# Block 2's gates: two more slots as three float32r products, and half of the states' turn back on GpSimd

## The reference, cut to what matters

```
h = rms_norm(x, mix_norm)
q_a, k_a, v_a, q_i, k_i, w_i, u_s, q_m, gates = split(h @ w_in)
...
bur, bui = einsum(u, bbr), einsum(u, bbi)          # inputs of the states
_, _, xr, xi = associative_scan(complex_affine, (ar, ai, bur, bui))
y = einsum(xr, c_re) - einsum(xi, c_im) + d * u
...
g = sigmoid(gates)                                 # 256 x 3 x 1024
merged = g[0] * o_a + g[1] * o_b + g[2] * o_m
```

## Time and profile before

| | |
|---|---|
| median of the runs | 2154.79 us (2153.62 to 2156.51) |
| the profiled execution | 2158.26 us, its span 2156.3 us |
| TensorE busy | 2119.3 us, 98% |
| VectorE, ScalarE, GpSimd busy | 74%, 56%, 8% |
| VectorE, low parts of the gates (L3084) | 2.29 us each |
| VectorE, turn of four states | six instructions of 1.22 us |
| VectorE, eight scans | 4.77 us |

### The profile page before, as it was taken

How to read it: one execution, slowest core, us unless ns; L and a number is a source line. 1 busy time by engine, 2 the same in 40 slices (tenths; PEclk the granted TensorE clock), 3 DMA queues, 4 the chain that set the end, 5 groups by cost and what they waited for, 6 DMA issues and landing times.

```text
span 2156.3 us, 31393 instructions
## 1 busy us (share of the span) xinstructions
PE 2119.3 (98%) x11893; PEld 1774.7 (82%) x11893; DVE 1588.5 (74%) x1653; ACT 1217.9 (56%) x1210; POOL 170.6 (8%) x240
## 2 busy tenths in 40 slices
PE   9999999999899999999999999999999999989998
PEld 8987888898788888888888888888788887877887
DVE  3676553567698989989898989989865539866454
ACT  4154443315477777777777777777664423664443
POOL 1200000320200000000000000000166010000000
PEclk9999999999999999999999999999999999999999
DMA  9134555523499999999999999999845564435562
GB/s 364 61 99 157 185 194 175 153 64 102 136 376 371 359 379 371 366 378 363 371 364 372 364 375 368 366 378 361 327 156 187 188 186 156 157 108 164 187 194 79
DMA packets 244409, 542.31 MB, mean 251 GB/s; under 512 B 20214, under 2 KB 122656, under 8 KB 243936
## 3 DMA queue, kind: packets, MB, share of 16 engines
q1 hardware_dynamic: 238896, 521.37, 67.4%
q0 software_dynamic: 4448, 13.79, 2.3%
q10 hardware_dynamic: 976, 5.91, 0.7%
HBM read 538.64 MB, written 2.36 MB: 251 GB/s over the span
## 4 chain that ended last, share of the span: by engine, by line
PE 92%; DVE 6%; ACT 1%; issue 1%; DMA 0%; DVEq 0%; SPq 0%; ACTq 0%
PE bank L1492 9%; PE bank L1493 9%; PE bank L1496 9%; PE bank L1339 9%; PE bank L1341 9%; PE bank L1340 9%; PE bank L1065 6%; PE bank L1520 5%; PE bank L1519 5%; PE bank L1524 5%; PE bank L1063 2%; PE bank L1658 2%; PE bank L1478 1%; PE bank L1132 1%; PE bank L1360 1%; PE bank L1151 1%
## 5 line engine op out<-in xcount | busy, mean ns | idle before, releaser
L2464 DVE TENSOR_TENSOR weights_lo<-ring_data,weights_hi 128x2048 fp32r<-128x2048 f32 x336 | 759.9, 2289 | 81.4 <-ACT weights_hi L2135 80.3
L2135 ACT ACTIVATE weights_hi<-ring_data 128x2048 fp32r<-128x2048 f32 x336 | 639.9, 1920 | 183.5 <-DMA ring_data<-in_moe_w 182.6
L1492 PE MATMUL bank<-weights_hi,xg_hi 128*128 128x512 f32 x896 | 351.6, 392 | 0.0
L1493 PE MATMUL bank<-weights_hi,xg_lo 128*128 128x512 f32 x896 | 348.9, 389 | 0.0
L2459 DVE TENSOR_TENSOR weights_lo<-ring_data,weights_hi 128x2048 fp32r<-128x2048 f32 x98 | 226.5, 2341 | 49.4 <-ACT weights_hi L1910 49.4
L1496 PE MATMUL bank<-weights_lo,xg_hi 128*128 128x512 f32 x896 | 239.8, 389 | 0.0
L1340 PE MATMUL bank<-weights_lo,xT_hi 128*128 128x512 f32 x584 | 230.2, 394 | 0.0
L1339 PE MATMUL bank<-weights_hi,xT_hi 128*128 128x512 f32 x520 | 206.9, 398 | 1.5 <-DVE xT_lo L2452 0.6
L1341 PE MATMUL bank<-weights_hi,xT_lo 128*128 128x512 f32 x520 | 203.8, 392 | 0.0
L1496 PEld LDWEIGHTS bank<-weights_lo,xg_hi 128*128 128x128 f32 x896 | 168.2, 188 | 35.1
L1493 PEld LDWEIGHTS bank<-weights_hi,xg_lo 128*128 128x128 f32 x896 | 168.3, 188 | 34.0
(11 more groups left out here) (524 smaller groups left out, 3181.8 us busy)
## 6 DMA issues: line engine op xcount, KB each, us to landing
ring_data<-in_moe_w SPq DMA_DIRECT2D x672, 512.0 KB, 4.6
ring_data<-in_ffn_w_in SPq DMA_DIRECT2D x88, 512.0 KB, 4.5
ring_data<-in_w_in SPq DMA_DIRECT2D x71, 512.0 KB, 4.3
ring_data<-in_ffn_w SPq DMA_DIRECT2D x66, 512.0 KB, 4.2
ring_data<-in_ffn_w_out SPq DMA_DIRECT2D x44, 512.0 KB, 4.0
ring_data<-in_w_out SPq DMA_DIRECT2D x24, 512.0 KB, 4.6
ring_data<-in_w_in SPq DMA_DIRECT2D x8, 396.0 KB, 4.2
ring_data<-in_w_in SPq DMA_DIRECT2D x8, 390.0 KB, 5.3
```

The costliest lines, as they stand in the source:

```text
L1492: mm(o, xg_hi[:, k, :], e_hi(at)[:, r], start=k == 0, stop=False)
L1493: mm(o, xg_lo[:, k, :], e_hi(at)[:, r], start=False, stop=False)
L2135: nc.scalar.activation(e_hi(at), ring_data[:, e_slot(at), :], ACT.Copy).then_inc(ring.hi_done, 1)
L2464: v.tensor_tensor(e_lo(at), ring_data[:, e_slot(at), :], e_hi(at), ALU.subtract).then_inc(ring.lo_done, 1)
```

## The change

- TensorE: slots 0 and 1 of the gates are three products too. Slot 0 takes the parts in the order hi·hi, hi·lo, lo·hi, as slot 2 did.
- ScalarE: `gate_high(0)` and `gate_high(1)` stand where `gate_high(2)` and `gate_high(3)` stood; these two come after the last projection and wait for slots 0 and 1.
- VectorE: after the last scans come `gate_low(0)`, `gx_lo` (which waits for the last projection), `gate_low(1)`, the turn back of the last four states, `gate_low(2)`, and then the selection.
- GpSimd: turns the first four states back, two at a time, after the first eight scans (`first_scanned`). Its temporaries lie in `qaT` and in unused room behind `rel`. TensorE's reading of the states, ScalarE's high parts of slots 9 and 11 and VectorE's squares of the queries wait for it (`states_turned`).

```diff
+            pool.wait_ge(sem("dve_stage"), stage("first_scanned"))
+            u0, u1, u2 = pool_tmp
+            for j in (0, 2):
+                js, gtt = slice(j, j + 2), nc.gpsimd.tensor_tensor
+                c, s, br, bi = Ct[:, js, :], St[:, js, :], bu[:, js, 0, :], bu[:, js, 1, :]
+                st.do(gtt(u0, br, s, ALU.mult))
+                st.do(gtt(u1, bi, s, ALU.mult))
+                st.do(gtt(u2, bi, c, ALU.mult))
+                st.settle()
+                st.do(gtt(br, br, c, ALU.mult))
+                st.settle()
+                st.do(gtt(br, br, u1, ALU.subtract))
+                i = gtt(bi, u2, u0, ALU.add)
+                if j == 0:
+                    st.do(i)
+                    st.settle()
+            i.then_inc(sem("pool_stage"), 1)
+            pool.wait_ge(sem("pool_stage"), stage("states_turned"))
...
                 def gate_slot(t):
-                    if t >= 2:
-                        pe.wait_ge(sem("gate_hi"), t - 1)
+                    pe.wait_ge(sem("gate_hi"), t + 1)
...
-                    if t < 2:
-                        ring2.arrived(pe, N_GATE + t)
-                        i = products(actT, ring2.slot(N_GATE + t).rearrange("p (k c) -> p k c", k=4), start=half == 0, stop=half == 1)
+                    products(gx_hi, w_hi, start=half == 0)
+                    if t == 0:
+                        pe.wait_ge(sem("gate_lo"), 1)
+                        products(gx_hi, w_lo)
+                        pe.wait_ge(sem("gx_lo"), 1)
+                        i = products(gx_lo, w_hi)
...
                 def gate_high(t):
-                    if t >= 4:
+                    if t >= 2:
                         act.wait_ge(ring2.used, N_GATE + t - 1)
...
-                gate_high(2)
+                gate_high(0)
...
-                gate_high(3)
+                gate_high(1)
...
+                for g in range(2):
+                    dve.wait_ge(sem("bu_act"), 4 * g + 4)
+                    st.do(turn_states(g, -1))
+                    st.settle()
+                    for j in range(4 * g, 4 * g + 4):
+                        m = q26[8][:, j:j + 1].broadcast_to([P, T])
+                        for q in range(2):
+                            i = v.tensor_tensor_scan(bu[:, j, q, :], m, bu[:, j, q, :], 0.0, ALU.mult, ALU.add)
+                            if (g, j, q) != (0, 3, 1):
+                                st.do(i)
+                            else:
+                                i.then_inc(sem("dve_stage"), 1)
+                    st.settle()
+                gate_low(0)
+                dve.wait_ge(sem("gx_hi"), 1)
+                dve.wait_ge(ring2.used, N_GATE)
+                v.tensor_tensor(gx_lo[:, :, :], actT[:, :, :], gx_hi[:, :, :], ALU.subtract).then_inc(sem("gx_lo"), 1)
+                gate_low(1)
+                turn_states(1, 1).then_inc(sem("dve_stage"), 1)
 
                 gate_low(2)
-                dve.wait_ge(sem("gx_hi"), 1)
-                dve.wait_ge(ring2.used, N_GATE + 2)
-                v.tensor_tensor(gx_lo[:, :, :], actT[:, :, :], gx_hi[:, :, :], ALU.subtract).then_inc(sem("gx_lo"), 1)
```

More of the change, by code:

```diff
@@ L523, in two_block_kernel @@
         row_bc = qmT[:, 0, :]
+        pool_tmp = (qaT[:, 0:2, :], qaT[:, 2:4, :], arena[:, at_att + 6 * T:at_att + 8 * T].rearrange("p (j c) -> p j c", j=2))
         kva, kd = ar(TT, P), ar(TT, P)
@@ L1651, in gate_slot @@
                         pe.wait_ge(sem("gate_out"), c - 1)
-                    if t >= 2:
-                        w_hi, w_lo = (w.rearrange("p (k c) -> p k c", k=4) for w in (gate_hi[t], gate_lo(t)))
+                    w_hi, w_lo = (w.rearrange("p (k c) -> p k c", k=4) for w in (gate_hi[t], gate_lo(t)))
                     def products(x, w, start=False, stop=False):
@@ L1659, in products @@
                         return i
-                    if t < 2:
-                        ring2.arrived(pe, N_GATE + t)
-                        i = products(actT, ring2.slot(N_GATE + t).rearrange("p (k c) -> p k c", k=4), start=half == 0, stop=half == 1)
-                    else:
[L1665 to L1674, removed]
+                    products(gx_hi, w_hi, start=half == 0)
[4 more added lines that the diff above has]
+                        i = products(gx_lo, w_hi)
+                    else:
+                        products(gx_lo, w_hi)
+                        pe.wait_ge(sem("gate_lo"), t + 1)
+                        i = products(gx_hi, w_lo, stop=half == 1)
                     i.then_inc(ring2.used, 1)
@@ L1712, in branches @@
                 project(6)
-                for t in range(2):
-                    gate_slot(t)
                 pe.wait_ge(sem("gx_hi"), 1)
-                for t in range(2, GATE_SLOTS - 2):
+                for t in range(GATE_SLOTS - 2):
                     gate_slot(t)
@@ L1781, in branches @@
                 pe.wait_ge(sem("dve_stage"), stage("states_ready"))
+                pe.wait_ge(sem("pool_stage"), stage("states_turned"))
                 pe.wait_ge(sem("gate_out"), GATE_CHUNKS)
@@ L2263, in gate_high @@
                         act.wait_ge(sem("dve_stage"), stage("states_ready"))
+                        act.wait_ge(sem("pool_stage"), stage("states_turned"))
                     nc.scalar.activation(gate_hi[t], ring2.slot(N_GATE + t), ACT.Copy).then_inc(sem("gate_hi"), 1)
@@ L2301, in branches @@
                 for c in range(GATE_CHUNKS - 1):
-                    if c:
-                        gate_high(2 * c + 2)
+                    gate_high(2 * c + 2)
                     if c == 3:
@@ L2306, in branches @@
                         a_(rq[:, :], ssq[:, :], ACT.Sqrt, "act_stage", scale=1.0 / HD, bias=NORM_EPS)
-                    if c:
-                        gate_high(2 * c + 3)
+                    gate_high(2 * c + 3)
                     gate_chunk(c)
@@ L3087, in branches @@
                 t0, t1, t2 = (turn_tmp[:, i] for i in range(3))
[L3088 to L3111, removed]
@@ new lines, in turn_states @@
+                def turn_states(g, sign):
+                    js = slice(4 * g, 4 * g + 4)
+                    c, s, br, bi = Ct[:, js, :], St[:, js, :], bu[:, js, 0, :], bu[:, js, 1, :]
+                    st.do(tt(t0, br, s, ALU.mult))
+                    st.do(tt(t1, bi, s, ALU.mult))
+                    st.do(tt(t2, bi, c, ALU.mult))
+                    st.do(tt(br, br, c, ALU.mult))
+                    st.settle()
+                    st.do(tt(br, br, t1, ALU.add if sign < 0 else ALU.subtract))
+                    return tt(bi, t2, t0, ALU.subtract if sign < 0 else ALU.add)
@@ L3144, in branches @@
                 proj2_out(dve, 6)
+                dve.wait_ge(sem("pool_stage"), stage("states_turned"))
                 st.do(tt(head_sq[:, :, 0:512], qa[:, :, :], qa[:, :, :], ALU.mult))
```

6 lines of the change are left out of this document (3 added, 3 removed).

## The result

The changed kernel takes 2165.47 us (median of six runs, 2163.94 to 2166.69) where before has 2155.48 (six runs, 2153.62 to 2157.88): a ratio of 1.0045, 95% interval 1.0035 to 1.0056, or +10.0 us. The forecast was 2165.6 us, and slower.

The account below looks back on a forecast made before the run. TensorE, 98% busy, bounds the kernel. VectorE's twelve losses of 12.96 less 2.64 give +10.3, the clock 0.5: +10.8 us on the median 2154.79 makes 2165.6 us; range 2158.1 to 2168.6.

Parts of the forecast that it names:

- TensorE's own work: Gates: slots 0 and 1 as three products, 5.44 instead of 6.67 us each, 2.46 us less if parts come in time.
- VectorE's own work: Before the selection: two more low parts (4.42 us), one turn with settling less (7.06), net -2.64 us.
- Twelve losses: Behind the first scans: each of GpSimd's twelve instructions costs VectorE 1.08 us, 12.96 in all.
- That a scan is held up: VectorE's scans beside GpSimd: assumed held up like an instruction with both tensors in SBUF, though no row showed it.
- The first rival: Scans go on beside GpSimd: about 8.1 losses, +6.1 us, or +3.3 with seven smaller ones; chance 0.16.
- Where the twelve fall: On VectorE: one GpSimd instruction behind each of six turn instructions and each of the first six scans.
- the second rival: GpSimd waits until VectorE pauses; both engines early by 2.6 to 2.8 us, time 2152.0; chance 0.08.
- 0.3 us of waiting in slot 2: If GpSimd waits for a pause: slot 2's low part, at 1816.8, keeps TensorE some 0.3 us.
- the wait of 9.26 instead of 11.4: TensorE in slot 0: a new wait of 11.4 us for the low part, from 1804.8 to 1816.2.
- The clock: TensorE after slot 0's wait: 6 us at half speed lose 3 us of matmuls, about 0.5 left after slot 4.
- The last rival: TensorE's clock stays low longer than 6 us, slots 0 to 2 late: up to 3 us more, 2168.6; chance 0.06.

Follow-up runs that it names:

- no_gpsimd_turn: The changed kernel without GpSimd's twelve instructions, the first four states left turned: stage 57.08 us, ratio to before 0.9984.
- gates_only: Slots 0 and 1 as three products, but VectorE turns all states back itself, GpSimd none: stage 65.36 us, ratio to before 1.0027.
- gpsimd_between: The changed kernel with GpSimd's twelve let go in groups behind the low parts of slots 3 to 7: stage 58.44 us, ratio to before 0.9997.
- gpsimd_late: The changed kernel with GpSimd's start behind slot 3's low part and its third temporary moved: stage 59.02 us, ratio to before 1.0002.
- gpsimd_only: The kernel before, slots 0 and 1 still fp32, with GpSimd turning the first four states back: stage 64.36 us, ratio to before 1.0022.
- gpsimd_24_small: The changed kernel with GpSimd's work in 24 instructions of 128x256 instead of twelve of 128x512: stage 68.44 us, ratio to before 1.0038.

## Why the prediction was right

**TensorE's own work**, -2.46: -2.37 for the stage without GpSimd. Right.

**VectorE's own work**, -2.64: together with the losses, 12.12 - 2.64 = 9.48; measured from the second turn's start to the selection's, 30.27 us before (1789.13 to 1819.40) and 39.72 after (1786.88 to 1826.60), +9.45. Right. Without GpSimd, in `no_gpsimd_turn`, the same stretch is 27.82 us, -2.45. The selection's start before:

```profile
1819.40 0.54 DVE L3124 TENSOR_SCALAR arena<-arena,small 128x128 f32<-128x128 f32 x2
```

**Twelve losses**: predicted 12 x 1.08 = 12.96, measured 12.12, 1.01 each. The row that gave 1.08 was one of 2.40 us beside low parts; its size was 7% too large. This is the mis-sized term, worth 0.84 of the 0.85 us between 10.3 and 9.45.

**That a scan is held up** was the open point, and the nearest row, the instruction on two full tensors in SBUF, was a good guide, though the scan has one of its two operands repeated: 1.02 us each. The first rival, in which scans go on beside GpSimd, falls.

**Where the twelve fall** was wrong in part. I had one behind each of the six turn instructions and of the first six scans, and named a turn at its old spacing of 1.14 as proof against me. The first four did keep it, the last two didn't. I had also called the turn and the scans queued without a gap; but VectorE settles behind the fourth multiplication, and it was there that GpSimd came in. Then two losses fell on the turn, eight on the scans, and the last two on the low part of slot 0 and `gx_lo`. The turn took 9.06 us, not over 12. The number of losses did not change, because there was enough VectorE work behind. So the second rival, GpSimd waiting for a pause, describes the entry rightly, but not what follows. (Its 0.3 us of waiting in slot 2 was a slip: by its own times the low part is there at 1816.8, and TensorE asks for it 3.6 us behind 1813.9, at 1817.5; `no_gpsimd_turn` has no wait there.) Where the losses fell also explains most of the wait of 9.26 instead of 11.4: the loss on `gx_lo`, 1.07, lies behind the low part that TensorE waits for, and 12 x 0.07 = 0.84 is the smaller loss: 1.9 of the 2.1.

**The clock**: back some 6 us after the restart, 2.85 us of matmuls lost (predicted 3). I had 0.5 of it in the sum; hardly any of it shows, since VectorE's delay of 9.45 still ends last in slot 4, with 0.34 us of waiting left. That this cover is what hides it is shown by `gates_only`, where it isn't there and 1.3 to 1.5 us come through. The last rival falls.

Sum: predicted +10.8; the stage has +9.53, the medians +10.0 (their interval, +7.5 to +12.1, holds both). The forecast of 2165.6 lay 0.1 us from the median, closer than the terms deserve, and that is luck: twelve losses and the clock were 0.85 and 0.4 too dear, against which stand some 0.5 us between stage and medians, within the runs' spread, and the median before, which came out 0.7 above the 2154.79 that I had added to.

## What to carry to other kernels

Work given to an idle GpSimd is not free while VectorE runs instructions with two inputs in SBUF: price each GpSimd instruction that reads SBUF at its own time less 0.2 to 0.3 us on VectorE (1.01 of 1.29 us here), and compare that with what VectorE is spared (12 us for 7 here). It costs nothing beside instructions that don't contend (here `max` and `match_replace`), so look for those, and then ask whether what waits for GpSimd can bear it that late. A faster TensorE stage gains only what its operands' maker can follow: here the low parts up to slot 6 came less than 1 us before their products, or behind them, and two cheaper slots needed two more low parts.

## What was not expected of the hardware

- In the change GpSimd did not get in between VectorE's four multiplications, which followed one another without a wait (5.57 us for its first, 2.16 with a settle behind each), but then took turns with the scans, which do follow one another so; and in `gpsimd_between` it got in between two squares without a wait, after a rest of 2.61 us. What distinguishes these cases is open.
- An instruction with one tensor in SBUF can be held up: the mask, a `tensor_scalar` of 128x384, took 1.28 us in `gpsimd_late` instead of 0.36. `max` and `match_replace` beside the same instructions lost nothing.
- TensorE's granted clock fell behind shorter waits too: 0.50 in the stretch from 1824 behind the 6.30 us of `gates_only`, at a price of 2.8 us for the two groups there, and 0.54 in the stretch from 1822 behind the 3.50 us of `gpsimd_only`. Behind slot 0's 3.33 us in `gpsimd_24_small` it stayed at 1.00.
